# A top-16 over 64 of 256 sums, one-hot matrices split over three engines, and two chunk loads moved ahead, in a conditioned decoder step

## What is computed

```python
s_top, i_top = lax.top_k(scores, PEER_TOPK)
cand = s_top[:, :, 0, :, None] + s_top[:, :, 1, None, :]
cand_idx = i_top[:, :, 0, :, None] * PEER_NKEYS + i_top[:, :, 1, None, :]
best, sel = lax.top_k(cand.reshape(T, PEER_HEADS, PEER_TOPK * PEER_TOPK), PEER_TOPK)
idx = jnp.take_along_axis(cand_idx.reshape(...), sel, axis=-1)
gates = jax.nn.softmax(best, axis=-1)
act = jax.nn.gelu(jnp.einsum('td,tkd->tk', xb, expert_u[ib]).astype(f32), approximate=False)
out = jnp.einsum('tk,tkd->td', (gb * act).astype(xb.dtype), expert_v[ib])
```

## Time and profile before

| | |
|---|---|
| Median of three runs | 2185.99 us (2184.54 to 2191.48) |
| Profiled execution | 2191.72 us, span 2189.5 |
| Busy over the span | TensorE 2010.9 (92%), VectorE 1567.2 (72%), ScalarE 858.7 (39%), GpSimd 747.3 (34%) |
| Choice block | 907 to 1204 us |
| Stages of quads, start to last product | 979.7 to 1049.9, 1055.4 to 1125.3, 1131.0 to 1192.9 us |
| TensorE clock over the span | 0.963 of full speed |

### The profile page before, as it was taken

How to read it: one execution, slowest core, us unless ns; L and a number is a source line. 1 busy time by engine, 2 the same in 40 slices (tenths; PEclk the granted TensorE clock), 3 DMA queues, 4 the chain that set the end, 5 groups by cost and what they waited for, 6 DMA issues and landing times. The chain is left out here.

```text
span 2189.5 us, 35793 instructions
## 1 busy us (share of the span) xinstructions
PE 2010.9 (92%) x13294; PEld 1754.8 (80%) x13294; DVE 1567.2 (72%) x3048; ACT 858.7 (39%) x1464; POOL 747.3 (34%) x687
## 2 busy tenths in 40 slices
PE   5989989999878799989787899999999999999996
PEld 3788889888767699747556888898898998899985
DVE  4465556655544568899785768888888888888886
ACT  3334333434331132419788333333333333333333
POOL 0010001110013023029887334444444545444540
PEclk9999999999988999999899999999999999999998
DMA  8611111111123222365457899999899999999991
GB/s 348 271 49 49 56 44 50 50 50 49 49 84 111 87 78 69 112 196 168 128 159 212 327 354 342 341 346 344 329 342 334 344 344 333 340 335 344 344 335 62
DMA packets 168063, 454.78 MB, mean 208 GB/s; under 512 B 15280, under 2 KB 71984, under 8 KB 164560
## 3 DMA queue, kind: packets, MB, share of 16 engines
q1 hardware_dynamic: 121808, 284.66, 37.4%
q0 software_dynamic: 46080, 167.79, 20.9%
HBM read 410.76 MB, written 41.63 MB: 207 GB/s over the span
## 5 line engine op out<-in xcount | busy, mean ns | idle before, releaser
L416 PE MATMUL pp<-act_hi,w_hi 128*128 128x272 f32 x1216 | 281.3, 313 | 47.6 <-DVE act_lo L1755 13.9
L2358 PE MATMUL pp<-act_hi,w_hi 128*128 128x384 f32 x800 | 272.3, 340 | 17.3 <-DVE w_lo L404 17.3
L2358 PE MATMUL pp<-act_lo,w_hi 128*128 128x384 f32 x800 | 270.3, 338 | 0.0
L2358 PE MATMUL pp<-act_hi,w_lo 128*128 128x384 f32 x800 | 269.7, 337 | 0.0
L416 PE MATMUL pp<-act_hi,w_lo 128*128 128x272 f32 x1216 | 255.9, 292 | 0.0
L416 PE MATMUL pp<-act_lo,w_hi 128*128 128x272 f32 x1216 | 255.8, 292 | 0.0
L416 PEld LDWEIGHTS pp<-act_hi,w_hi 128*128 128x128 f32 x1216 | 193.4, 193 | 70.5 <-issue 30.8
L400 ACT ACTIVATE w_hi<-w_raw 128x1024 fp32r<-128x1024 f32 x176 | 185.1, 1051 | 100.4 <-PE pp L416 82.5
L2129 POOL TENSOR_SCALAR hot_b<-cst,gcols 128x128 f32<-128x128 f32 x288 | 193.7, 691 | 42.8 <-DVE gcols L2143 42.1
L908 POOL TENSOR_TENSOR lm<-lt,cst 128x512 f32<-128x512 f32 x40 | 57.7, 1443 | 438.8 <-DVE lt L1356 318.5
L404 DVE TENSOR_TENSOR w_lo<-w_raw,w_hi 128x1024 fp32r<-128x1024 f32 x162 | 199.0, 1228 | 9.1 <-ACT w_hi L400 9.0
(11 more groups left out here) (363 smaller groups left out, 4210.6 us busy)
## 6 DMA issues: line engine op xcount, KB each, us to landing
w_raw<-in_stream SPq DMA_DIRECT2D x204, 512.0 KB
v_raw<-in_v SPq DMA_DIRECT2D x128, 512.0 KB
ada_w<-in_ada SPq DMA_DIRECT2D x24, 1024.0 KB, 11.5
gate_matrix<-gstage SPq DMA_DIRECT2D x12, 2048.0 KB, 9.3
gt<-gate_matrix SPq DMA_DIRECT2D x32, 768.0 KB
early<-cst SPq DMA_DIRECT2D x28, 192.0 KB
cst<-early SPq DMA_DIRECT2D x28, 192.0 KB
s_s<-in_delta SPq DMA_DIRECT2D x8, 512.0 KB, 7.2
```

The lines of the kernel that those rows point to most:

```text
L416: last = nc.tensor.matmul(pp[s][:, b, 0:HN], w[:, c * P:(c + 1) * P], a[:, c, b * HN:(b + 1) * HN], start=(c == 0 and w is w_hi[s] and a i ...
L2358: last = nc.tensor.matmul(pp[s][:, 0, 0:TD], w[:, c * P:(c + 1) * P], a[:, c, 0:TD], start=(c == 0 and w is w_hi[s] and a is act_hi), stop ...
```

## The change

The choice adds only the pairs with (i + 1)(j + 1) at most 16 and some more, 64 in four rectangles: row 0 with 16 columns, rows 1 to 3 with 8, rows 4 to 7 with 4, rows 8 to 15 with 1. `top16` runs over 64 elements, and row and column are decoded from the cell number with nine small operations in seven dependent steps. `beside` is called once more.

Of a quad, all four `hot_b` come from one VectorE operation of 512 elements; `hot_a` of tokens 0 and 1 from GpSimd (compare and multiply by the gate), of token 2 from VectorE, of token 3 from ScalarE. TensorE writes product o to every fourth word of the bank from word o on, so that ScalarE stores runs of four words instead of single ones.

SyncE loads the first two chunks of the expert block in the place of the early chunks 28 and 29, and ScalarE splits the first one at the end of the choice block.

```diff
+CELLS = 64
...
-        cand_less = at("cand_less", 46 * K, [P, H, TOPK * TOPK])
+        sums, sums_less = at("sums", 46 * K, [P, H, CELLS]), at("sums_less", 48 * K, [P, H, CELLS])
+        sel_p, dec = at("sel_p", 50 * K, [P, 3, H, TOPK]), [at(f"dec{n}", 52 * K + 512 * n, [P, H, TOPK]) for n in range(2)]
...
+            else:
+                sp.wait_ge(e_done, i - 1)
+                load_chunk(sp, Chunk(C_U + i - NE))
...
-                            for which in range(q % 2, 2):
-                                last = nc.scalar.activation(away[:, 2 * (q % 2) + which, :], iota, ACT.Abs,
-                                                            bias=gcols[:, which, c:c + 1], scale=-1.0)
-                            last.then_inc(away_done, 1)
+                            nc.scalar.activation(away[:, q % 2, :], iota, ACT.Abs, bias=gcols[:, 0, c:c + 1],
+                                                 scale=-1.0).then_inc(away_done, 1)
...
-                            if q % 2 == 0:
-                                nc.scalar.activation(hot_a[:, v, :], away[:, 2 * (q % 2), :], ACT.Relu,
-                                                     bias=gcols[:, 2, c:c + 1], scale=gcols[:, 3, c:c + 1])
-                            nc.scalar.activation(hot_b[:, v, :], away[:, 2 * (q % 2) + 1, :], ACT.Relu, bias=one[:],
-                                                 scale=-1.0).then_inc(hot_c_ready, 1)
+                            nc.scalar.activation(hot_a[:, v, :], away[:, q % 2, :], ACT.Relu, bias=gcols[:, 2, c:c + 1],
+                                                 scale=gcols[:, 3, c:c + 1]).then_inc(hots_scalar, 1)
...
-                    out = gstage[s][:, :, 4 * (q % NQ):4 * (q % NQ) + 4].rearrange("p j t -> p t j")
-                    nc.scalar.activation(out, dd[:, q % 4, :].rearrange("p (t j) -> p t j", t=4),
+                    nc.scalar.activation(gstage[s][:, :, 4 * (q % NQ):4 * (q % NQ) + 4],
+                                         dd[:, q % 4, :].rearrange("p (j t) -> p j t", t=4),
...
+                for s in range(2):
+                    act.wait_ge(turn_st[s], 16 * 4)
+                split_hi(act, Chunk(C_U))
...
-                            last = nc.tensor.matmul(dd[:, q % 4, o * P:(o + 1) * P], hot_a[:, v, :], hot_b[:, v, :],
-                                                    start=True, stop=True)
+                            last = nc.tensor.matmul(dd[:, q % 4, o::4], hot_a[:, v, :], hot_b[:, v, :], start=True, stop=True)
...
-                        for o in range(3):
+                        for o in range(2):
                             c = 4 * q + o
-                            last = nc.gpsimd.tensor_scalar(hot_b[:, (q % HOTS) * 4 + o, :], iota, gcols[:, 1, c:c + 1],
-                                                           None, ALU.is_equal)
-                        last.then_inc(hot_b_ready, 1)
+                            last = nc.gpsimd.tensor_scalar(hot_a[:, (q % HOTS) * 4 + o, :], iota, gcols[:, 0, c:c + 1],
+                                                           gcols[:, 2, c:c + 1], ALU.is_equal, ALU.mult)
+                        last.then_inc(hots_pool, 1)
...
-                    for o in range(3 + q % 2):
-                        c = 4 * q + o
-                        last = nc.vector.tensor_scalar(hot_a[:, (q % HOTS) * 4 + o, :], iota, gcols[:, 0, c:c + 1],
-                                                       gcols[:, 2, c:c + 1], ALU.is_equal, ALU.mult)
-                    last.then_inc(hot_a_ready, 1)
+                    v, c = (q % HOTS) * 4, 4 * q
+                    nc.vector.tensor_tensor(hot_b[:, v:v + 4, :], iota.unsqueeze(1).to_broadcast([P, 4, P]),
+                                            gcols[:, 1, c:c + 4].unsqueeze(2).to_broadcast([P, 4, P]), ALU.is_equal)
+                    nc.vector.tensor_scalar(hot_a[:, v + 2, :], iota, gcols[:, 0, c + 2:c + 3], gcols[:, 2, c + 2:c + 3],
+                                            ALU.is_equal, ALU.mult).then_inc(hots_vector, 1)
...
-                    a = pair[:, hs_, 0, :].unsqueeze(3).to_broadcast([P, nh, TOPK, TOPK])
-                    b = pair[:, hs_, 1, :].unsqueeze(2).to_broadcast([P, nh, TOPK, TOPK])
-                    st(nc.vector.tensor_tensor(cand[:, hs_], a, b, ALU.add))
+                    a, b = pair[:, hs_, 0, :], pair[:, hs_, 1, :]
+                    for at, i0, ni, nj in ((0, 0, 1, 16), (16, 1, 3, 8), (40, 4, 4, 4), (56, 8, 8, 1)):
+                        st(nc.vector.tensor_tensor(
+                            sums[:, hs_, at:at + ni * nj].rearrange("p h (i j) -> p h i j", j=nj),
+                            a[:, :, i0:i0 + ni].unsqueeze(3).to_broadcast([P, nh, ni, nj]),
+                            b[:, :, 0:nj].unsqueeze(2).to_broadcast([P, nh, ni, nj]), ALU.add))
...
-                    flat = cand[:].rearrange("p h a b -> p h (a b)")
-                    top16(dve, st, lambda j: flat[:, j, :], lambda j: cand_less[:, j, :], lambda j: best[:, j, :],
+                    top16(dve, st, lambda j: sums[:, j, :], lambda j: sums_less[:, j, :], lambda j: best[:, j, :],
...
-                    st(nc.vector.tensor_scalar(sel_ab[:, 0, hs_], sel[:, hs_], 4, None, ALU.logical_shift_right))
-                    st(nc.vector.tensor_scalar(sel_ab[:, 1, hs_], sel[:, hs_], 15, None, ALU.bitwise_and))
+                    for n, shift in enumerate((3, 2)):
+                        st(nc.vector.tensor_scalar(sel_ab[:, n, hs_], sel[:, hs_], shift, None, ALU.logical_shift_right))
+                    st(nc.vector.tensor_copy(sel_p[:, 2, hs_], sel[:, hs_]))
                     st.settle()
-                    st(nc.vector.tensor_copy(sel_f[:, :, hs_], sel_ab[:, :, hs_]))
+                    st(nc.vector.tensor_copy(sel_p[:, 0:2, hs_], sel_ab[:, :, hs_]))
+                    beside()
+                    eighth, quarter, cell = (sel_p[:, n, hs_] for n in range(3))
+                    row, col, d0, d1 = sel_f[:, 0, hs_], sel_f[:, 1, hs_], dec[0][:, hs_], dec[1][:, hs_]
+                    st(nc.vector.tensor_scalar(d0, cell, -48.0, 0.0, ALU.add, ALU.max))
+                    st.settle()
+                    st(nc.vector.scalar_tensor_tensor(out=d0, in0=quarter, scalar=-6.0, in1=d0, op0=ALU.add, op1=ALU.max))
+                    st.settle()
+                    st(nc.vector.scalar_tensor_tensor(out=row, in0=eighth, scalar=-1.0, in1=d0, op0=ALU.add, op1=ALU.max))
+                    st.settle()
+                    st(nc.vector.tensor_scalar(d0, row, 4.0, 24.0, ALU.mult, ALU.add))
+                    st(nc.vector.tensor_scalar(d1, row, 8.0, 8.0, ALU.mult, ALU.add))
+                    st.settle()
+                    st(nc.vector.scalar_tensor_tensor(out=d0, in0=row, scalar=48.0, in1=d0, op0=ALU.add, op1=ALU.min))
+                    st(nc.vector.scalar_tensor_tensor(out=d1, in0=row, scalar=16.0, in1=d1, op0=ALU.mult, op1=ALU.min))
+                    st.settle()
+                    st(nc.vector.tensor_tensor(d0, d0, d1, ALU.min))
+                    st.settle()
+                    st(nc.vector.tensor_tensor(col, cell, d0, ALU.subtract))
...
-                sp.wait_ge(e_done, NE)
-                for j in range(2):
-                    load_chunk(sp, Chunk(C_U + j))
...
-                split_hi(act, Chunk(C_U))
```

More of the change, by code:

```diff
@@ L321, in build @@
         hot_a = at("hot_a", 62 * K, [P, 4 * HOTS, P])
-        away = at("away", 70 * K, [P, 4, P])
+        away = at("away", 70 * K, [P, 2, P])
         hot_b = nc.alloc_sbuf_tensor_at("hot_b", [P, 4 * HOTS, P], F32, offset=split_base + 8 * K)
@@ L1961, in build @@
             sem("p5_dve"), sem("ex_in"), sem("ex_out"), sem("picks_ready"), sem("picks_tr"), sem("chosen"))
-        gcols_ready, hot_a_ready, hot_b_ready, hot_c_ready, away_done, quad_done, quad_read = (
-            sem("gcols_ready"), sem("hot_a_ready"), sem("hot_b_ready"), sem("hot_c_ready"), sem("away_done"),
+        gcols_ready, hots_vector, hots_pool, hots_scalar, away_done, quad_done, quad_read = (
+            sem("gcols_ready"), sem("hots_vector"), sem("hots_pool"), sem("hots_scalar"), sem("away_done"),
             sem("quad_done"), sem("quad_read"))
@@ L2087, in quads @@
                     for q in range(n // 4):
-                        pe.wait_ge(hot_a_ready, u * TQ + (q + 1))
-                        pe.wait_ge(hot_b_ready, u * TQ + (q + 1))
-                        pe.wait_ge(hot_c_ready, u * TQ + (q + 1))
+                        pe.wait_ge(hots_vector, u * TQ + (q + 1))
+                        pe.wait_ge(hots_pool, u * TQ + (q + 1))
+                        pe.wait_ge(hots_scalar, u * TQ + (q + 1))
                         pe.wait_ge(quad_read, u * TQ + (q + 1))
```

## The result

The changed kernel takes 2193.2 us (median of 20 runs) against 2187.0 of the kernel before (20 runs): ratio 1.0030 with a 95% interval of 1.0018 to 1.0042. It is slower by about 6 us, where 19 less were forecast. The profiled executions have spans of 2194.6 and 2189.5, 5.1 apart.

A forecast was written before the change was run, and what follows sets the result against it. GpSimd's 96 compares were taken to pace all three stages, TensorE's early chunks the time before. Terms 0 - 7.3 - 7.0 - 3.4 - 1.5 + 0 = -19.2 us gave a forecast of 2167 us, range 2152 to 2198.

The forecast's parts named there:

- GpSimd's sum: First stage: GpSimd's 64 builds, wide-compare holds and four long operations take 59.0 us against 67.1, so GpSimd stops being the bound.
- The price X: Stages: one GpSimd build with two column pointers and a multiply, taken as 0.68 us between 0.598 and 1.20.
- The hold by a wide compare: Stages: each quad's wide VectorE compare delays GpSimd by 0.24 us, 7.7 us for 32.
- Rival 1: Stages: GpSimd stays the bound at 64 X + 15.5; 2223 us at X = 1.0; chance 0.13, 0.24 with its band.
- the band of no change: Part of rival 1: GpSimd's build costs 0.75 to 0.85 us, nothing measurable remains, 2186 us; chance 0.11.
- The floor: Stages: VectorE's late part sets the first two, 62.9 us to the last product; TensorE the third, 58.5.
- The first two choices: Before the first stage: their 14 us saved only lengthen VectorE's wait behind TensorE's early chunks; 0, bounds -4 to +4.
- The strided write: Stages: products written to every fourth word of PSUM, taken at no cost, ceiling 1.0 us a quad.
- rival 2: Stages: the strided write slows the products; at the ceiling some 2250 us; chance 0.10.
- The store: Behind each stage's last product: ScalarE's store in runs of four takes 0.5 us less, three times, -1.5.
- Rival 3: Before the stages: the choices' 14 us come through too, giving 2153 us; chance 0.04.
- rival 4: Stages: VectorE waits more and they gain only half, 2177 us; counted within the forecast's 0.62.

The follow-up runs named there:

- the kernel without a GpSimd limit: Changed kernel with a compare alone on GpSimd (gate of tokens 0 and 1 left out) and the iota row in PSUM for the wide compare: 2173.6 us, one run.

## Why the prediction was wrong, point by point

**What bounds the kernel** was right: GpSimd in the stages, TensorE's early chunks before them. The kernels that take time off GpSimd shorten the stages until it falls to some 60 us, and the one with the row in PSUM gains what was forecast for the whole change.

**The failed step is GpSimd's sum**, "43.5 + 7.7 + 7.8 = 59.0 against 67.1", and with it the sentence that GpSimd stops being the bound. In the first stage it is 70.7. The price X was set at 0.68 after ScalarE's surcharge for a pointer; it is 0.787, since the second operation costs as well: 64 x 0.107 = 6.9 us. The hold by a wide compare was taken as 0.24, from five operations of the third stage; it is 0.34: 3.3 us. The four long operations hold for 9.3 us (59.7 - 64 x 0.787), not 7.8. Together 11.7, which is the whole difference between 59.0 and 70.7.

**Both holds were small by a reading of the kernel before.** The forecast took 96 x 0.598 = 57.4 us off GpSimd's busy time and called the rest holds. But the records of builds that follow each other overlap a little:

```profile
1152.64 5.83 POOL L2129 TENSOR_SCALAR hot_b<-cst,gcols 128x128 f32<-128x128 f32 x10
...
1166.66 1.10 POOL L2129 TENSOR_SCALAR hot_b<-cst,gcols 128x128 f32<-128x128 f32 x1
1166.70 0.68 DVE L2187 TENSOR_TENSOR cand<-sel_f,cst 128x512 f32<-128x512 f32 x1
```

Ten undisturbed builds take 5.83 us, so each comes 0.58 behind the last. 96 of them are 55.4 us (0.577 each), and the holds are 3.2 us of the third stage instead of 1.2. The one shown is 0.50, and the five builds beside the five tensor_tensors of that stage are 0.50, 0.50, 0.33, 0.58 and 0.33 over their 0.60: 0.45 each and not 0.24. In the first stage the rest is 11.7 instead of 9.7, 2.3 for each long operation instead of 1.94. Read so, with a build 0.08 dearer than 0.577, the forecast's sum would have been 64 x 0.66 + 32 x 0.45 + 4 x 2.3 = 65.8, close to the 67.1 of before, without any second operation's price. (The same overlap is in the 64 x 0.787 above, where builds come 0.775 apart: it moves 0.8 us from the price to the long holds and leaves the sum.)

**Rival 1 is what happened**, but not by its own formula. 64 X + 15.5 at the measured 0.787 gives 65.9, under today's 67.1; the 0.81 at which it reaches today's pace was not reached. The holds did the rest. The measured mean hold of 0.34 lies between the forecast's 0.24 and the 0.53 of the rival; with 0.24 and the measured price GpSimd would be at 50.4 + 7.7 + 9.3 = 67.4, which is the pace of before. The rule of the Trainium skill that was weighed there (SBUF — State Buffer, Who interferes with whom) is borne out here: a second input in SBUF makes the hold and its removal ends it, and in the single operations above the later of the two stands until the earlier is through, with 0.52 us over where they start together. The rival's 0.53 for every compare is not, since many compares meet a build partway, which makes the mean 0.34. The forecast set the rule aside with the 0.24 of its misread row. I had left the rule inside the band of no change, without adding a dearer X to it; that the two could fall together is what the range lacked. The range contains the 2193 of the result; the direction was wrong.

**The floor** was right in size: VectorE's late part and TensorE were to end the stages at 62.9, 62.9 and 58.5; the kernel without a GpSimd limit has 63.3, 65.2 and 59.5, the second 2.3 longer than forecast. (The forecast's terms for the last pair add up to 61.6 and not to 61.8.) The experiments do not tell VectorE's late part from TensorE's own time in it, save that five more pieces a stage (ten more records) lengthen all three in the PSUM kernel.

**The other terms.** The first two choices: taken as 0, and it was 0; moving two chunks shows the 10 us beneath. VectorE's wait grew to 12.5 and not to 17, because the second choice took 31.3 us (934.67 to 965.98) and not 27.4: VectorE stood idle in it for 2.63 us before 946.67, which the profile puts down to a DMA and the kernel before does not have there, for 0.89 shortly before, and for 0.58 behind the exp, which came after an early chunk's gelu. What held VectorE for the first two is open. An undisturbed full choice is 27.4 us (907.28 to 934.67), 7 less, as worked out. The strided write: 0, as taken; rival 2 is refuted, and with it, for 32-bit products of 128 columns, the rule of the Trainium skill (PSUM — Partial Sum Buffer, Specifications (TRN2)) that non-contiguous patterns slow matmuls. The store: 0.48 less, and the chain behind a stage 5.1 us instead of 5.5. The moved loads: 0 forecast, 0.7 measured. Rival 3 fell, rival 4 does not arise.

**From GpSimd's time to the stage.** GpSimd is 3.6 us longer in the first stage and the stage 4.1; in the third, 3.8 and 2.3. TensorE's granted clock plays a small part in this. It is 0.89 in the first stage of the changed kernel, 0.93 in the kernel before and 1.00 in the PSUM kernel: TensorE has the lower of its two levels, 1.2 GHz in place of 2.4, for 17.0 of 74.3 us, and had it for 10.2 of 70.3 before. One such stretch is

```profile
1034.30:1041.10 6.80, 5.72 (x20) 4.00 (x19) 6.80 (x7) 2.54 (x6) 6.80 (x6) 0.50 0.88 266
```

and the products at 1037.63 above take 2.05 us in it instead of 1.05. But GpSimd never waited for TensorE, so a slow product can only lengthen the piece between GpSimd's last build and the last product. That piece is 3.5, 1.8 and 1.7 us in the changed kernel and was 3.0, 1.2 and 3.3: 0.5 and 0.6 longer, then 1.5 shorter. The 9.3 us of the stages are GpSimd's.

**The better version** is the changed kernel with its iota row in PSUM for the wide compare: 0.9912 of the kernel before, 19 us below it, and below the changed kernel by 23 us by the medians and 26 by the two ratios. These 19 us are what was forecast for the change; the place of one operand gives them.

## What to carry to other kernels

Where an engine paces a stage, count for each operation moved beside it both what the new form costs (measure it once: here a second operation and a second pointer made 0.60 into 0.79 us) and what the other engines' new operations hold up. Read a hold from the single operation beside it, or take the undisturbed pace from a run of operations (ten in 5.83 us) and not from the length of one record, which here made 0.45 us into 0.24. A wide two-input VectorE operation beside a busy GpSimd is not free; giving it one operand from PSUM took the hold away at no cost to VectorE. And before pricing a shorter chain, see what the next wait would be: here 14 us of choice lay wholly behind TensorE's chunks.

## What the runs showed of the hardware that was not expected

- GpSimd's tensor_scalar over 128 columns: 0.597 us for a compare with one column pointer, 0.708 with a multiply by an immediate, 0.787 with a multiply by a second column.
- VectorE's 512-element tensor_tensor with both inputs in SBUF costs a busy GpSimd 0.34 us in the mean (32 of them 11.0) and 0.52 where both start together; if GpSimd's operation started first, the tensor_tensor takes up to 0.84 us. With one input in PSUM it costs GpSimd nothing that the median shows (790 ns against a shortest of 783) and takes 0.69 us.
- TensorE's 32-bit products of 128 columns take the same time written to every fourth word of a bank as to neighbouring words (286 and 287 ns a record).
- ScalarE's copy of 512 words takes 1.08 us when each word goes to a place of its own 128 bytes from the last, and 0.60 in runs of four.
